# Gates of one token tile: one-hot products on TensorE replaced by scattered additions into a cleared table in DRAM

## What is computed

```python
q = einsum('td,de->te', xc, wq)                 # 8 heads, 2 halves of 128
s = einsum('thpd,hpnd->thpn', q, sub_keys)      # 128 keys a half
sv, si = top_k(s, 16)
cand = sv[:, :, 0, :, None] + sv[:, :, 1, None, :]
cidx = si[:, :, 0, :, None] * 128 + si[:, :, 1, None, :]
top, pos = top_k(cand, 16)
eidx = take_along_axis(cidx, pos)               # 16 experts a head, of 16384
g = softmax(top)
a = gelu(einsum('thkd,td->thk', u[eidx], xc))
y = einsum('thk,thkd->td', g * a, v[eidx])
```

## Time and profile before

| | us |
|---|---|
| median of 3 runs | 1540.63 (1540.01 to 1541.29) |
| the profiled execution | 1543.53 |
| its span from first to last instruction | 1541.7 |
| around the span | 1.8 |
| TensorE busy in the span | 1489.7 (97%) |
| VectorE | 1277.7 (83%) |
| ScalarE | 710.9 (46%) |
| GpSimd | 617.1 (40%) |
| 96 groups of one-hot products, TensorE | 102.5 |

### The profile page before, as it was taken

The page is one execution under the profiler, slowest core; times in us unless marked ns, Lnnn a source line. Parts: engine busy times, 40 slices in busy tenths (PEclk is TensorE's granted clock), DMA queues, the critical chain, the costliest instruction groups (busy, mean ns, idle before and its releaser), DMA issues.

```text
span 1541.7 us, 24351 instructions
## 1 busy us (share of the span) xinstructions
PE 1489.7 (97%) x8276; PEld 1325.4 (86%) x8276; DVE 1277.7 (83%) x2494; ACT 710.9 (46%) x1409; POOL 617.1 (40%) x508
## 2 busy tenths in 40 slices
PE   4999999999998999999899999999999999999997
PEld 4877777888898999999899999999999988888886
DVE  5788665689998979889759888889899988888787
ACT  3444553233345747567544444444444434443433
POOL 1121300033461424344246555556767655455300
PEclk9999999999999999999999999999999999999999
DMA  9754320133355888989899999999999999999962
GB/s 365 274 171 163 136 84 1 41 97 95 98 179 163 272 253 269 297 251 325 252 357 397 337 363 359 352 356 363 385 395 385 376 364 411 384 379 387 348 242 96
DMA packets 164099, 417.14 MB, mean 271 GB/s; under 512 B 12697, under 2 KB 70169, under 8 KB 163873
## 3 DMA queue, kind: packets, MB, share of 16 engines
q1 hardware_dynamic: 95936, 244.88, 44.5%
q0 software_dynamic: 41472, 151.01, 25.9%
q10 hardware_dynamic: 26594, 20.05, 4.0%
HBM read 376.57 MB, written 38.80 MB: 269 GB/s over the span
## 4 chain that ended last, share of the span: by engine, by line
PE 79%; DVE 16%; DMA 2%; ACT 2%; issue 1%; ACTq 0%; DVEq 0%; SPq 0%
PE bank_S L1061 16%; PE bank_T L1061 11%; PE bank_G L1061 5%; PE bank_T L1039 5%; PE bank_O L1001 5%; PE bank_O L1003 5%; PE bank_O L1002 5%; PE bank_S L1001 3%; PE bank_S L1003 3%; PE bank_S L1002 3%; PE bank_O L761 2%; PE bank_S L728 2%; DVE mod_acc L2221 2%; DVE mod_acc L2191 2%; DVE v_sb L2197 1%; DVE v_sb L2184 1%
## 5 line engine op out<-in xcount | busy, mean ns | idle before, releaser
L1673 ACT ACTIVATE v_hi<-v_raw 128x1024 fp32r<-128x1024 f32 x124 | 131.6, 1061 | 287.0 <-PE bank_G L1061 278.7
L1642 ACT ACTIVATE u_hi<-u_raw 128x1024 fp32r<-128x1024 f32 x128 | 135.4, 1058 | 211.5 <-PE bank_O L1003 107.3
L2465 DVE TENSOR_TENSOR v_lo<-v_raw,v_hi 128x1024 fp32r<-128x1024 f32 x124 | 152.1, 1227 | 87.8 <-ACT v_hi L1673 63.1
L1001 PE MATMUL bank_S<-h_hi,u_hi 128*128 128x352 f32 x576 | 196.3, 341 | 7.9 <-DVE u_lo L2299 2.7
L1393 POOL DMA_INDIRECT row<-in_peer_v,stage x128 | 177.0, 1383 | 42.2 <-issue 37.5
L1393 POOL DMA_INDIRECT row<-in_peer_u,stage x128 | 146.3, 1143 | 104.3 <-POOL stage L1389 99.8
L1002 PE MATMUL bank_S<-h_lo,u_hi 128*128 128x352 f32 x576 | 186.3, 323 | 0.0
L2455 DVE SCALAR_TENSOR_TENSOR y<-row,wgt,y 128x1024 f32<-128x1024 f32 x128 | 164.5, 1285 | 0.0
L2481 DVE SCALAR_TENSOR_TENSOR row<-row,h 128x1024 f32<-128x1024 f32 x128 | 156.2, 1221 | 0.0
L1001 PE MATMUL bank_O<-h_hi,u_hi 128*128 128x352 f32 x448 | 145.2, 324 | 0.0
L1002 PE MATMUL bank_O<-h_lo,u_hi 128*128 128x352 f32 x448 | 144.3, 322 | 0.0
(11 more groups left out here) (436 smaller groups left out, 3938.7 us busy)
## 6 DMA issues: line engine op xcount, KB each, us to landing
u_raw<-in_u_t SPq DMA_DIRECT2D x128, 512.0 KB
v_raw<-in_peer_v SPq DMA_DIRECT2D x128, 512.0 KB
g_in<-gates SPq DMA_DIRECT2D x32, 768.0 KB
ada_late<-in_w_ada SPq DMA_DIRECT2D x8, 2048.0 KB, 8.2
gates<-g_out SPq DMA_DIRECT2D x8, 2048.0 KB, 11.6
spill<-a_act ACTq DMA_DIRECT2D x64, 176.0 KB
a_act<-spill SPq DMA_DIRECT2D x16, 704.0 KB
w_raw<-in_w_in SPq DMA_DIRECT2D x20, 512.0 KB, 4.0
```

Of the source, the lines that this page charges most:

```text
L1001: pe.matmul(ps[:, 0:DX], u_hi[q][:, kk], h_hi[:, k, GT * P:S - XT], start=(k == 0), stop=False)
L1642: act.activation(u_hi[c % 2][:, :], u_raw[:, c % 2, :], ACT.Copy).then_inc(s_uhi, 1)
L1673: act.activation(v_hi_end[:, i % TAIL, :] if end else v_hi[:, c % 2, :], v_raw[c % 4][:, :], ACT.Copy)\
L2465: dve.tensor_tensor(lo[:, q, :], v_raw[c % 4][:, :], hi[:, q, :].bitcast(f32), ALU.subtract)\
```

## The change

Tile 2 (128 tokens, blocks 4 to 7) no longer goes through one-hot products. Its four blocks of the table are cleared during attention by 16 transfers of 512 KB from a small field of zeros. Tile 2 is decoded first, ahead of tile 3; VectorE turns each of its 128 x 128 pairs into a place in the table (`scatter_places`), and GpSimd issues 128 indirect transfers, each of which adds 128 single values, one a partition, at the places. Before each sixteenth it waits until all earlier ones have landed, since a later head may name a place again. 12 are issued at once, the others between its splits and gathers by a written table, `SCAT_BESIDE`. SP's load of the first piece of the table waits for all 128. The phases go from four to three, the gaps are longer, and the products of the last 32 tokens move along.

```diff
-PHASES = [[8, 9, 10], [0, 1, 2, 3], [4, 5, 6, 7], [X_BLOCK]]
-PHASE_TILE = [3, 1, 2, 3]
-GAPS = [23, 7, 6, 6]
+SCAT_TILE = 2
+SCAT_BLOCKS = slice(4, 8)
+ZERO_PIECES = 16
+PHASES = [[8, 9, 10], [0, 1, 2, 3], [X_BLOCK]]
+PHASE_TILE = [3, 1, 3]
+GAPS = [28, 9, 13]
...
-DOTS_AFTER = {30: 1, 31: 1, 32: 1, 45: 1, 46: 1, 47: 1, 58: 3, 59: 2, 60: 2}
+DOTS_AFTER = {39: 2, 40: 2, 41: 1, 51: 2, 52: 3, 53: 3, 54: 3, 55: 3, 56: 2}
...
+SCAT_FIRST = 12
+SCAT_BESIDE = dict([(i, 3) for i in range(28, 51)] + [(i, 1) for i in range(51, 57)] + [(i, 3) for i in range(57, 64)]
+                   + [(64, 4), (65, 4)] + [(i, 3) for i in range(66, 70)])
...
             sp.dma_start(x_sb[:, :, :], x[0].rearrange("(t p) d -> p t d", p=P)).then_inc(s_x, 16)
+            sp.wait_ge(s_zero, 4)
+            for n in range(ZERO_PIECES):
+                step = NCHUNK // 4 // ZERO_PIECES
+                sp.dma_start(gates[:, step * n:step * n + step, SCAT_BLOCKS, :, :].rearrange("p q b i t -> p q (b i t)"),
+                             zeros[:, :].unsqueeze(1).to_broadcast([P, step, 512])).then_inc(s_cleared, 16)
...
             unit_done(sp, 19)
+            sp.wait_ge(s_cleared, 16 * ZERO_PIECES)
...
                     sp.wait_ge(s_gfirst, 16)
+                    sp.wait_ge(s_scat, 16 * P)
                     load_g(0, 0, False)
...
+            def scatter(first, end):
+
+                for n in range(first, min(end, P)):
+                    if n % TOPK == 0 and n:
+                        pool.wait_ge(s_scat, 16 * n)
+                    pool.indirect_dma_start(gate_places, bass.IndirectOffsetOnAxis(place_u[:, n:n + 1], 0),
+                                            gate[:, SCAT_TILE, n:n + 1], None, compute_op=ALU.add).then_inc(s_scat, 16)
+
+            pool.wait_ge(s_cleared, 16 * ZERO_PIECES)
+            pool.wait_ge(s_xidx, 1)
+            scattered = SCAT_FIRST
+            scatter(0, scattered)
+            pool.wait_ge(s_xidx, 1 + QUARTERS)
             got = 2
             gather_x(0, got)
-            for phase, blocks in enumerate(PHASES):
-                for i in range(BESIDE[blocks[0]], BETWEEN[phase + 1].start + 1):
-                    ready = dots_before(i - 2) + X_PLACES
-                    if blocks[-1] != X_BLOCK:
-                        ready = min(ready, got + 2)
-                    gather_x(got, ready)
-                    got = max(got, ready)
+            for i in range(BESIDE[PHASES[0][0]], EARLY):
+                if i in LOW_ON_POOL:
                     split_u(i, i)
+                ready = dots_before(i - 1) + X_PLACES
+                gather_x(got, ready)
+                got = max(got, ready)
+                scatter(scattered, scattered + SCAT_BESIDE.get(i, 0))
+                scattered += SCAT_BESIDE.get(i, 0)
...
+                if J == 30:
+                    dve.wait_ge(s_accd, 12)
+                    dve.memset(zeros[:, :], 0.0).then_inc(s_zero, 1)
...
+            def scatter_places():
+
+                i_key, j_key = key_f[:, SCAT_TILE, 0, :], key_f[:, SCAT_TILE, 1, :]
+                done(dve, dve.tensor_copy(quarter_u[:, :], i_key), s_dv)
...
+                dve.scalar_tensor_tensor(out=place_u[:, :], in0=quarter_f[:, :], scalar=float(4 * (DT - GB)),
+                                         in1=place_f[:, :], op0=ALU.mult, op1=ALU.add).then_inc(s_xidx, 1)
...
                     first = FIRST_LOW + 3
-                    decode(NT - 1, s_dv, [([first], [], [first + 1]), ([], [first + 2], [])])
+                    decode(SCAT_TILE, s_dv, [([first], [], [first + 1]), ([], [first + 2], [])])
                     normalise()
+                    scatter_places()
+                    split_and_dot(first + 3)
+                    decode(NT - 1, s_idx, [([first + 4], [], [first + 5]), ([], [first + 6], [])])
                     index_x()
```

More of the change, by code:

```diff
@@ L245, in peer_block_kernel @@
         gate = at("gate", 198, [P, NT, PH * TOPK])
+        zeros = at("zeros", 96, [P, 512])
+        place_u = at("place_u", 62, [P, P], u32)
+        quarter_u = at("quarter_u", 62.5, [P, P], u32)
+        quarter_f = at("quarter_f", 63, [P, P])
+        place_f = at("place_f", 63.5, [P, P])
         onehot = at("onehot", 48, [P, TOPK, PH * TOPK], bf16)
@@ L1016, in last_and_columns @@
                 else:
-                    pe.wait_ge(s_idx, phase + 1)
+                    pe.wait_ge(s_idx, phase + 2)
                     for n, m in enumerate((key_f[:, tile, 1, :], key_f[:, tile, 0, :], gate[:, tile, :])):
@@ L1799, in _ @@
                         stored += 1
-                    if phase == len(PHASES) - 2 and n == len(gap) - 4:
+                    if phase == len(PHASES) - 2 and n == len(gap) - 6:
                         gelu_of_x()
                     if i == EARLY - 2:
-                        act.wait_ge(s_gst[0], 16 * stores_of(BLOCKS - 2))
+                        act.wait_ge(s_gst[0], 16 * stores_of(ORDERED - 2))
                         v_high(0, 0)
@@ L1978, in _ @@
             mod_row(5)
-            dve.wait_ge(s_const, 8)
+            dve.wait_ge(s_const, 9)
+            for q in range(1, QUARTERS):
+                part = slice(GB * q, GB * q + GB)
+                done(dve, dve.tensor_scalar(token_at[part, :], token_at[part, :], float(q * (P - GB)), None, ALU.add),
+                     s_dv)
             def soft_in(J):
@@ L2373, in _ @@
                     first = FIRST_LOW + 3
-                    decode(NT - 1, s_dv, [([first], [], [first + 1]), ([], [first + 2], [])])
+                    decode(SCAT_TILE, s_dv, [([first], [], [first + 1]), ([], [first + 2], [])])
                     normalise()
+                    scatter_places()
+                    split_and_dot(first + 3)
+                    decode(NT - 1, s_idx, [([first + 4], [], [first + 5]), ([], [first + 6], [])])
                     index_x()
-                    rest = list(range(first + 3, BETWEEN[0].stop))
+                    rest = list(range(first + 7, BETWEEN[0].stop))
                 else:
@@ L2382, in _ @@
                     if phase == len(PHASES) - 1:
-                        for n in rest[0:2]:
+                        for n in rest[0:6]:
                             split_and_dot(n)
-                        rest = rest[2:]
+                        rest = rest[6:]
                         decode(0, s_idx, [(rest[0:1], [], rest[1:2]), ([], rest[2:3] + [None], [])])
```

45 lines of the change are left out of this document (28 added, 17 removed).

## The result

The changed kernel takes 1619.5 us (median of four runs, 1618.8 to 1621.3) against 1540.7 of the kernel before, a ratio of 1.051 with a 95% interval of 1.050 to 1.053. I had forecast 1532. TensorE has less work and waits longer.

What follows compares the result with a forecast made beforehand. TensorE was taken as the stage's bound, with GpSimd setting the pace from unit 28 to 65 after the change. 28.5 + 4.1 - 20.2 - 4.0 = 8.4 us less, median 1532.2 us; own range 1524 to 1537.

Steps and rivals of the forecast that it cites:

- What goes from TensorE: Blocks of the stage: 32 one-hot groups at 0.89 us, 28.5 us, plus a phase start of 4.1 us; at most 32.6.
- The price of an addition: GpSimd, units 28 to 65: 104 additions at the common gather's 1.25 us with issue, ends 0.94 and 2.05.
- dearer: Rival on GpSimd: a third descriptor per value makes an addition 1.48 us with issue, 24 us over forecast, 1556 us; chance 0.26.
- long ones: GpSimd: 6 additions slowed beside VectorE's decodes at 0.8 us each, 4.8 us.
- The exposed waits: GpSimd, units 28 to 65: five waits for landings with nothing between, 2.0 us each, 10.0 us; landing 3.0 us from issue.
- the balance: Units 28 to 65: GpSimd's 227.8 us of work against TensorE's 203.6 plus 4.0 slack, so TensorE waits about 20.2 us.
- The first wait at unit 43: Sign in the trace: TensorE waits for GpSimd's low parts, first at unit 43.
- The end of the stage: Behind unit 66: last 12 additions and a landing delay the table's first piece and units 71 and 72's loads; 4 us, ends 0 and 8.
- Costed at nothing: `scatter_places`' six small operations, an earlier decode, the clearing and merged semaphores: 0; 2 us if cover goes, clearing's ends 0 and 9.
- The DMA engines: Rival between blocks: 4-byte packets, read and write counted apart, overfill the engines; 9 us over forecast, 1541 us; chance 0.09.
- All covered: Rival: an addition takes 1.10 us and lands in 2.0, TensorE never waits for GpSimd; 1510 us; chance 0.16.
- The clearing: Rival: the table's clearing during attention comes too late, output weights wait, 9 us, 1541 us; chance 0.03.

Runs made afterwards that it cites:

- without additions: Changed kernel with the 128 additions and SyncE's wait for them left out; clearing, places and order kept: 1514.7 us, ratio 0.983.
- plain writes: Changed kernel with the addition taken off the 128 scattered transfers, so each overwrites its place; waits kept: 1551.0 us.
- half tile, last: Changed kernel with only tile 2's last 64 tokens by 64 additions, re-placed, table's first piece asked for ahead of unit 73's load: 1533.8 us.
- moving the wait: Changed kernel with SyncE's wait for the last addition and the table's first load put behind the loads of units 71 and 72: 1609.9 us.
- half tiles: Five versions of the changed kernel, 64 additions for tile 2's last 64 tokens, one-hot for the first 64: 1550.0, 1550.3, 1539.4, 1535.2, 1533.8 us.

## Why the prediction was wrong

The mechanism of the forecast, GpSimd's work set against TensorE's pace, is what the runs show. What failed is above all one term of it, the price of an addition; the waits for landings and the end of the stage were also too small.

*What goes from TensorE* was nearly right. I gave 28.5 + 4.1 us, and 2 back at the end, so 1510 us where all is covered; without additions it is 1514.7. Trace against trace the stage lost 30.0 us (386.2 to 356.1), where 30.6 was forecast. Most of the 4.7 us lies outside it: about 1 us ahead of the stage (below), 0.4 behind it, and some 2.5 because the traced execution of the kernel before stood 2.9 us above its median and this one's 0.4. Loads of `u_raw` come late between the blocks (units 40, 52, 54 and 55 took 5.2 to 7.9 us instead of 3.9), which I had not counted and did not test alone, but the stage as a whole shows little of it.

*The price of an addition* is the step that failed most: the term of 104 additions at the price of the common gather. I took 1.25 us with the issue, and it is 1.85 (mean 1.91), inside my bounds of 0.94 and 2.05 but far from the row I chose. Against plain writes it is worth 68.5 us of the 87.3 that the forecast is off. I had seen the mechanism as a rival, "dearer", and weighed it 0.26; its reason, a descriptor more for each number, was wrong, and its size of 1.48 us too. That it too has 128 addresses to work out compared what both share and left out the one thing in which they differ. I had also put 4.8 us on long ones. In the changed kernel 15 additions took over 1.8 us, each beside an operation of VectorE with two inputs in SBUF, splits as well as bf16 comparisons; 18 of the 105 ordinary ones lay beside such an operation too, so what makes one long is not shown. All that the additions took over their median is 11 us.

*The exposed waits* were 10 us in the sum and are 21.8, six of them with a mean of 3.6 us. The sixth is the one that I had read behind two gathers, the 48th: it stands directly behind an addition (624.65 and 629.46 us in the timeline above), and the gathers come three additions later. From the issue of one addition to the start of the next that waited for its landing it is 4.2 to 7.2 us, 5.3 in the mean, and not 3: it lies between the 2.0 us of the earlier trace rows and the 7.6 of the earlier trace rows. Why is not shown.

With these two the balance is right, and so is the rule "GpSimd sets the pace". The forecast's own sum at the measured prices is 45.5 + 30 x 1.25 + 104 x 1.91 + 21.8 = 303.4 us, against 297.8 measured; with it and the 18 us for the end (below) the time would have come to 1622 us. From the gelu of unit 27 to that of 65, us (GpSimd's work summed from its timeline, gaps of issue and landings in it; the last column is how long it waited for high parts; without additions it waits 28 us more for VectorE to free rows):

```
kernel               units 27 to 65   GpSimd's work   waits for u_hi
no additions              212.8           81               102
plain writes              241.0          239                 2
all additions             297.8          308                 0
half tile, last           227.2          194                37
```

With plain writes GpSimd's 239 us and its 2 us of waits are the time of the stretch. With additions the sum is 308, but a split that follows an addition starts 0.55 us ahead of its end; take 18 x 0.55 off and 298 stand, the whole stretch: GpSimd is never idle for want of a high part. My sum had 227.8. Without additions the stretch takes 212.8 us, where I had 203.6 for TensorE and 4 more of slack.

*The first wait at unit 43* did not come true: the greatest is there, 29.9 us instead of a few, but TensorE waits for GpSimd's low parts before it, 4.7 us at unit 29, 1.5 at unit 32 and 3.3 at unit 34. Beside the blocks too, three additions and a split (5.55 + 2.5 us) are already more than the 7.42 us of a unit:

```profile
541.12 0.63 PE L1018 MATMUL bank_S<-h_hi,u_hi 128*128 128x352 f32 x1 [4.69 <-POOL h_lo L1402]
```

*The end of the stage* was 4 us with ends 0 and 8. It is 18 us: units 65 to 72 take 48.9 us with additions and 30.9 without. I wrote that SyncE holds two loads of u back, and still took 4 us for the whole. The 9.6 us that moving the wait gave is the part of the queue behind it.

*Costed at nothing:* the clearing costs nothing; the changed kernel is 2.3 us behind the one before both ahead of it, at 90 us, and behind it, at 416. Three small operations on `token_at`, which I did not name, stand on VectorE ahead of a softmax at 79 us. TensorE waits 1.66 us for that softmax where it waited 0.99, and behind this wait its granted clock is 0.50 from 82 to 85 us, where the kernel before has 1.00. So the next softmax starts 2.0 us later (86.19 us against 84.18), and VectorE waits 1.90 us for TensorE ahead of it. Eight other kernels with the same operations there kept the full clock at this place, so part of the 2.3 us is not theirs in every trace:

```profile
78.82 0.51 DVE L2022 TENSOR_SCALAR token_at<-token_at 32x1 f32<-32x1 f32 x3
...
86.19 0.35 DVE L2037 CUSTOM_DVE_ANT_0 Sb<-bank_S,dist_w,nsinks 128x128 f32<-128x128 f32 x1 [1.90 <-PE bank_S L745]
```

With them moved the gelu of unit 0 starts at 413.6 to 414.5 us in five kernels (mean 414.0), without at 414.4 to 416.3 in eleven (mean 415.3): some 1.3 us, in the mean. The five are the half tiles, which differ in other edits as well.

*The DMA engines* as a bound were a rival of 0.09 and did not come: TensorE's waits are for low parts, a packet took 38 ns and not twice 37, and additions with 32 packets in place of 144 gain no more than their shorter issue explains. *All covered* (1510) is what no additions at all nearly give, 1514.7. *The clearing* as a rival did not come either.

## What to carry to other kernels

Price a new kind of instruction by what sets it apart from the nearest row; where that is an operation no row shows, give the dear bound the weight, above all when the engine that gets the work has a break-even close to the cheap one (1.33 against 1.25 us here). An engine that waits half its time is not half free: it has what is left of each unit before the next consumer, so sum its work for the stretch and set it beside the pace, and move no more than leaves it waiting (37 us here). A wait on a DMA costs what is queued behind it, on GpSimd the next split and on SyncE the next loads: put it behind them.

## What the runs showed of the hardware

- An indirect transfer that adds takes GpSimd 1.55 us for 128 numbers, 1.40 for 64 and 1.34 for 8; a plain write or a gather by the same 128 numbers 0.95 to 0.96, of 4 bytes or of 4 KB a number. The next one starts 0.30 us behind its end.
- An addition of 128 numbers is 144 packets in GpSimd's queue, one of 8 is 32, and so is a plain write of 128.
- A split of 128x1024 that follows an addition at once starts 0.53 to 0.56 us before the addition's record ends and takes 2.91 to 2.97 us instead of 2.39. Behind a plain write it starts 0.02 to 0.17 us after the record's end and takes 2.35 to 2.41.
- Scattered plain writes into eight tables in DRAM made the same kernel some 29 us slower than into one, with loads that ScalarE used up to 12 to 20 us behind their issue.
- The granted clock fell while TensorE idled. Two windows of the changed kernel, in the 29.9 us and behind them: 0.50 of 2.4 GHz, and full again. From 650 to 655 us, in which TensorE takes up work at 653.68, it is still 0.50, and in the five us before 660 it is 0.63.

```profile
640.00:645.00 5.00, 0.00 (x0) 0.00 (x0) 0.00 (x0) 0.00 (x0) 4.09 (x4) 0.50 0.33 41
...
660.00:665.00 5.00, 5.00 (x39) 5.00 (x38) 4.74 (x9) 3.92 (x9) 4.53 (x4) 1.00 0.31 53
```
